# Decoder layer on one core: the SwiGLU up-projection by eight block products, or by seven

## The reference

```python
h = rms_norm(x, g_ffn[l])
u = h @ w_up[l]                      # (256, 2048) @ (2048, 11264)
up = jnp.pad(u, ((0, 0), (CONV_WIDTH - 1, 0), (0, 0)))
conv = sum(wc[t] * up[:, t:t + s] for t in range(CONV_WIDTH)) + b_conv[l]   # 3 taps along the tokens
gate, val = jnp.split(conv, 2, axis=-1)                                      # 5632 columns each
x = x + (jax.nn.silu(gate) * val) @ w_down[l]                                # (256, 5632) @ (5632, 2048)
```

## Time and profile before

| | |
|---|---|
| median of three runs | 1414.6 us |
| profiled execution, first to last instruction | 1413.1 us |
| PE busy | 1405.8 us (99%) |
| DVE busy | 890.7 us (63%) |
| ACT busy | 722.2 us (51%) |
| POOL busy | 53.0 us (4%) |
| moved by DMA | 265.97 MB, 188 GB/s on the mean |

### The profile page before, as it was taken

How to read it: one execution, slowest core, us unless ns; L and a number is a source line. 1 busy time by engine, 2 the same in 40 slices (tenths; PEclk the granted TensorE clock), 3 DMA queues, 4 the chain that set the end, 5 groups by cost and what they waited for, 6 DMA issues and landing times.

```text
span 1413.1 us, 19396 instructions
## 1 busy us (share of the span) xinstructions
PE 1405.8 (99%) x6947; PEld 1184.9 (84%) x6947; DVE 890.7 (63%) x1109; ACT 722.2 (51%) x884; POOL 53.0 (4%) x65
## 2 busy tenths in 40 slices
PE   8999999999999999999999999999999999999999
PEld 7888888888888888888888888888888888888887
DVE  5646455655454456555577767676767676776765
ACT  6655444464545444444555554555454645554551
POOL 0112111110000000000000000000000000000000
PEclk9999999999999999999999999999999999999999
DMA  9865555556666655756566666666666665656652
GB/s 332 257 188 162 160 160 167 170 165 189 181 188 183 189 188 187 239 182 194 176 194 182 198 185 187 190 189 189 188 185 193 179 195 176 203 170 206 178 191 93
DMA packets 138441, 265.97 MB, mean 188 GB/s; under 512 B 10528, under 2 KB 10784, under 8 KB 137888
## 3 DMA queue, kind: packets, MB, share of 16 engines
q1 hardware_dynamic: 135488, 262.36, 60.7%
q10 hardware_dynamic: 2912, 3.06, 0.7%
HBM read 263.29 MB, written 2.10 MB: 188 GB/s over the span
## 4 chain that ended last, share of the span: by engine, by line
PE 99%; DMA 0%; DVE 0%; SPq 0%; ACT 0%; issue 0%
PE acc L327 22%; PE acc L307 20%; PE acc L309 20%; PE acc L308 20%; PE acc L324 12%; PE acc L323 1%; PE acc L348 0%; PE acc L336 0%; PE acc L359 0%; PE acc L375 0%; DMA raw<-w_in 0%; PE acc L368 0%; PE acc L437 0%; PE acc L376 0%; PE acc L356 0%; PE acc L362 0%
## 5 line engine op out<-in xcount | busy, mean ns | idle before, releaser
L815 DVE TENSOR_TENSOR w_lo<-raw,w_hi 128x1024 fp32r<-128x1024 f32 x487 | 593.7, 1224 | 466.5 <-ACT w_hi L568 463.6
L568 ACT ACTIVATE w_hi<-raw 128x1024 fp32r<-128x1024 f32 x487 | 513.5, 1058 | 558.9 <-PE acc L309 372.6
L327 PE MATMUL acc<-actB,w_hi 128*128 128x512 f32 x1320 | 466.9, 398 | 0.0
L307 PE MATMUL acc<-w_hi,actA 128*128 128x512 f32 x1116 | 442.3, 396 | 2.0 <-DVE w_lo L815 2.0
L309 PE MATMUL acc<-w_hi,actA 128*128 128x512 f32 x1116 | 435.1, 390 | 0.0
L308 PE MATMUL acc<-w_lo,actA 128*128 128x512 f32 x1116 | 434.4, 389 | 0.0
L324 PE MATMUL acc<-actB,w_lo 128*128 128x256 f32 x1408 | 391.9, 281 | 0.0
L327 PEld LDWEIGHTS acc<-actB,w_hi 128*128 128x128 f32 x1320 | 248.0, 188 | 60.4
L324 PEld LDWEIGHTS acc<-actB,w_lo 128*128 128x128 f32 x1408 | 265.9, 189 | 2.0
L309 PEld LDWEIGHTS acc<-w_hi,actA 128*128 128x128 f32 x1116 | 209.5, 188 | 44.4
L307 PEld LDWEIGHTS acc<-w_hi,actA 128*128 128x128 f32 x1116 | 209.7, 188 | 43.7 <-issue 2.4
(11 more groups left out here) (141 smaller groups left out, 591.6 us busy)
## 6 DMA issues: line engine op xcount, KB each, us to landing
raw<-w_up SPq DMA_DIRECT2D x176, 512.0 KB, 4.2
raw<-w_in SPq DMA_DIRECT2D x159, 512.0 KB, 3.9
raw<-w_down SPq DMA_DIRECT2D x88, 512.0 KB, 4.5
raw<-w_out SPq DMA_DIRECT2D x32, 512.0 KB, 4.5
raw<-w_fox SPq DMA_DIRECT2D x16, 512.0 KB, 4.5
raw<-w_dil SPq DMA_DIRECT2D x16, 512.0 KB, 4.5
work<-x_t SPq DMA_DIRECT2D x8, 256.0 KB, 6.7
work<-x SPq DMA_DIRECT2D x2, 1024.0 KB, 8.9
```

What stands on the lines that cost most here:

```text
L307: nc.tensor.matmul(o, lhsT=a_h, rhs=w_hi[:, u, k, :], start=first and k == 0, stop=False)
L327: mm = nc.tensor.matmul(banks[j][:, :], lhsT=hi_w, rhs=actB[:, kt, :], start=False, stop=kt == KT - 1)
L568: nc.scalar.activation(w_hi[:, u, :, :], raw[:, u % RAW_SLOTS, :].rearrange("p (k n) -> p k n", k=KU), ACT.Copy).then_inc(hi_done, 1)
L815: nc.vector.tensor_tensor(w_lo[:, u, :, :], raw[:, u % RAW_SLOTS, :].rearrange("p (k n) -> p k n", k=KU), w_hi[:, u, :, :].bitcast(f32), A ...
```

## The change

The up-projection of a block is one product of 2 by 2 blocks. On the left stands the normalised input without its per-token factor, cut into two halves of tokens and two halves of the 2048 inner elements (A11, A12, A21, A22, each 128 by 1024). On the right stand four weight blocks of 1024 by 512: B11 and B21 (value columns, first and second half of the inner elements), B12 and B22 (gate columns). The seven products of Strassen's method, in the order of the new `step` 0 to 6, take A11, A12, S1, S4, S2, S3 and A22 on the left, where S1 to S4 are sums of the A blocks, made once. The weight sums on the right are made in place: SP loads B11 into `raw` and B21, later B22, into the new `raw_y`, and POOL issues DMAs that add a further block to what lies in the buffer (`accum_op=ALU.add`), for the steps 2, 4, 5 and 6. PE keeps on accumulating in the same PSUM bank over several steps, where the method allows it; ACT copies intermediate sums out (`p1_copied`, `p15_copied`, `p6_copied`), and DVE makes the four results of a block (`result`).

A unit of such a step ("S") has 6 matmuls of 512, with 128 tokens as the stationary operand, so that the tokens now lie on the partitions. The results are turned by 8 PE transposes for the gate and 8 for the value (`turn_up`), and all three taps are taken from PSUM. The down units ("D", 12 matmuls as before) are placed between the S units by a list, `ffn_units`. A block has 28 S and 8 D units: 36 weight units pass through `high` and `low` where 24 did. The D unit (i, 0) stands before S unit 12 of block i + 1. The first block has no D unit beside it, and after the last S unit 13 D units are left. The ring of split weights holds 6 units (`RING`), was 8. The whole program is unrolled. The arrays `w_up` and `w_down` are laid out so that a unit is contiguous, 4 KB on each partition. The last four attention heads no longer have their queries and values copied by POOL, and ACT's function tables are loaded once for the whole FFN, where before a block had two loads.

```diff
+STEPS = 7
+QU = HK // KU
+EARLY = (1, 4, 7)
+LATE = (12, 16, 20, 24, 26)
+LAST_LATE = 3
+X_STEPS = (0, 2, 4, 6)
+Y_STEPS = (1, 3, 5)
+
...
+def ffn_units():
+
+
+    units = []
+    for i in range(BLOCKS):
+        for step in range(STEPS):
+            for q in range(QU):
+                t = QU * step + q
+                late = LATE if i < BLOCKS - 1 else LATE[:LAST_LATE]
+                if i > 1 and t in EARLY:
+                    units.append(("D", i - 2, UPR - len(EARLY) + EARLY.index(t)))
+                if i > 0 and t in late:
+                    units.append(("D", i - 1, late.index(t)))
+                units.append(("S", i, step, q))
+    units += [("D", BLOCKS - 2, u) for u in range(LAST_LATE, UPR)]
+    units += [("D", BLOCKS - 1, u) for u in range(UPR)]
+    return units
+
+
...
+            def load_b11(i, q):
+                sp.dma_start(raw[:, q, :], w_up[1, i, q, :, :]).then_inc(w_loaded[q], 16)
+
+            def load_b21(i, q):
+                sp.dma_start(raw_y[:, q, :], w_up[1, i, QU + q, :, :]).then_inc(y_loaded[q], 16)
+
+            def load_b22(i, q):
+                sp.dma_start(raw_y[:, q, :], w_up[0, i, QU + q, :, :]).then_inc(y_loaded[q], 16)
+
+            def load_down(k):
+                sp.dma_start(raw_d[:, k % 2, :], w_down[k // UPR, k % UPR, :, :]).then_inc(d_loaded[k % 2], 16)
...
+            for n, unit in enumerate(FFN, FF_UNIT):
+                if unit[0] == "D":
+                    k = UPR * unit[1] + unit[2]
+                    if k + 2 < UPR * BLOCKS:
+                        sp.wait_ge(lo_done, n)
+                        load_down(k + 2)
...
+                    load_down(0)
+                    load_down(1)
+                if step == 1:
+                    sp.wait_ge(lo_done, n)
+                    load_b22(i, q)
+                elif step == 5 and i + 1 < BLOCKS:
+                    sp.wait_ge(lo_done, n)
+                    load_b21(i + 1, q)
+                elif step == 6 and i + 1 < BLOCKS:
+                    sp.wait_ge(lo_done, n)
...
+            def product_unit(n, part, q, o, first):
+
+                pe.wait_ge(lo_done, n)
+                s = n % RING
                 for k in range(KU):
-                    kt = KU * u + k
-                    for j in range(CT):
-                        hi_w, lo_w = w_hi[:, u, k, j * P:(j + 1) * P], w_lo[:, u, k, j * P:(j + 1) * P]
-                        if kt == 0:
-                            nc.tensor.matmul(banks[j][:, :], lhsT=hi_w, rhs=actB[:, kt, :], start=True, stop=False)
-                        mm = nc.tensor.matmul(banks[j][:, SEQ:], lhsT=lo_w, rhs=actB[:, kt, 0:SEQ],
-                                              start=False, stop=False)
-                        if kt > 0:
-                            mm = nc.tensor.matmul(banks[j][:, :], lhsT=hi_w, rhs=actB[:, kt, :], start=False,
-                                                  stop=kt == KT - 1)
+                    kt = KU * q + k
+                    a_h, a_l = part[:, kt, 0:P], part[:, kt, P:2 * P]
+                    nc.tensor.matmul(o, lhsT=a_h, rhs=w_hi[:, s, k, :], start=first and kt == 0, stop=False,
+                                     skip_group_check=True)
+                    nc.tensor.matmul(o, lhsT=a_h, rhs=w_lo[:, s, k, :], start=False, stop=False,
+                                     skip_group_check=True)
...
+            def turn_up(rows, ready):
+
+                for j in range(CT):
+                    for r in range(RT):
+                        t = nc.tensor.transpose(bank[3 + j // 2][:, (j % 2) * SEQ + r * P:(j % 2) * SEQ + (r + 1) * P],
+                                                rows[r][:, j * P:(j + 1) * P], ident)
+                t.then_inc(ready, 1)
+
+            def turn_val(i):
+                pe.wait_ge(c11_done, i + 1)
+                pe.wait_ge(c21_done, i + 1)
+                pe.wait_ge(conv_done, 2 * i + 1)
+                turn_up(val, val_ready)
+
+            def turn_gate(i):
+                pe.wait_ge(c12_done, i + 1)
+                pe.wait_ge(c22_done, i + 1)
+                if i:
+                    pe.wait_ge(conv_done, 2 * i)
+                turn_up(gate, gate_ready)
...
+            def down_unit(n, i, u):
+                c = u // 2
+                if u == 0:
+                    pe.wait_ge(a_lo, i + 1)
+                if u % 2 == 0:
...
+            for n, unit in enumerate(FFN, FF_UNIT):
+                if unit[0] == "D":
+                    down_unit(n, unit[1], unit[2])
...
+                if step == 0 and q == 2 and i:
+                    turn_val(i - 1)
+                elif step == 6 and q == 0:
+                    turn_gate(i)
...
+            def high(n):
...
+                    src = raw_d[:, u % 2, :]
+                    act.wait_ge(d_loaded[u % 2], 16 * (4 * i + u // 2 + 1))
+                else:
+                    _, i, step, q = FFN[n - FF_UNIT]
+                    src = raw[:, q, :] if step in X_STEPS else raw_y[:, q, :]
+                    if step == 0:
+                        act.wait_ge(w_loaded[q], 16 * (FF_UNIT // RAW_SLOTS + i + 1))
+                    elif step in X_STEPS:
+                        act.wait_ge(x_summed[q], 16 * (3 * i + step // 2))
+                    elif step == 5:
+                        act.wait_ge(y_summed[q], 16 * (i + 1))
+                    else:
+                        act.wait_ge(y_loaded[q], 16 * (2 * i + (step + 1) // 2))
+                if n >= RING:
+                    act.wait_ge(used, n - RING + 1)
+                nc.scalar.activation(w_hi[:, n % RING, :, :], src.rearrange("p (k n) -> p k n", k=KU),
                                      ACT.Copy).then_inc(hi_done, 1)
...
+            for n, unit in enumerate(FFN, FF_UNIT):
+                high(n + RING)
...
+                if step == 0 and q == 0 and i:
+                    gate_silu(i - 1)
+                elif step == 0 and q == 3:
+                    act.wait_ge(used, n + 1)
+                    if i:
+                        act.wait_ge(val_ready, i)
+                    else:
+                        act.wait_ge(nrs_ready, 1)
+                    for r in range(RT):
+                        t = nc.scalar.activation(val[r], bank[0][:, :], ACT.Copy, scale=xrs2[:, r:r + 1])
+                    t.then_inc(p1_copied, 1)
+                    if i:
+                        newest_tap(i - 1, 1)
+                elif step == 1 and i == 0:
...
+                elif step == 2 and q == 0 and i:
+                    hidden_high(i - 1)
...
+                elif step == 6 and q == 1:
+                    newest_tap(i, 0)
...
+            def older_tap(i, side, tap):
+
+                q = 2 * i + side
+                ct = 4 * i + 44 * side
+                if tap == 1:
+                    dve.wait_ge(tap2, q + 1)
+                else:
+                    dve.wait_ge(tap1, q + 1)
+                lag = 2 - tap
+                for j in range(CT):
+                    t = nc.vector.scalar_tensor_tensor(
+                        out=conv[:, j, lag:SEQ], in0=bank[3 + j // 2][:, (j % 2) * SEQ:(j % 2 + 1) * SEQ - lag],
+                        scalar=smalls_sb[:, S_WC + 88 * tap + ct + j:S_WC + 88 * tap + ct + j + 1],
+                        in1=conv[:, j, lag:SEQ], op0=ALU.mult, op1=ALU.add)
+                t.then_inc(tap1 if tap else conv_done, 1)
...
+                nc.vector.scalar_tensor_tensor(out=part, in0=o, scalar=scale, in1=part, op0=ALU.mult, op1=ALU.add)\
+                    .then_inc(done, 1)
+
+            for n, unit in enumerate(FFN, FF_UNIT):
+                low(n + RING)
+                if unit[0] == "D":
+                    _, i, u = unit
                     if u % 2 == 1:
-                        add_down(FF0 + 3 + 3 * i, u // 2)
...
+                if step == 1 and q == 3:
+                    dve.wait_ge(used, n + 1)
+                    dve.wait_ge(p1_copied, i + 1)
+                    result(bank[1][:, :], xrs2[:, 0:1], val[0], c11_done)
...
+                elif step == 6 and q == 2:
+                    older_tap(i, 0, 1)
+                elif step == 6 and q == 3:
+                    dve.wait_ge(used, n + 1)
+                    result(bank[2][:, :], xrs2[:, 1:2], val[1], c21_done)
+                    older_tap(i, 0, 0)
+                elif step == 1 and q < 3 and i:
+                    if q < 2:
+                        older_tap(i - 1, 1, 1 - q)
+                    else:
+                        hidden(i - 1)
+                elif step == 2 and q == 1 and i:
+                    hidden_low(i - 1)
 
...
+            def add_up(step, i, q):
+
+                if step in X_STEPS:
+                    half, side = {2: (0, 0), 4: (1, 0), 6: (1, 1)}[step]
+                    nc.gpsimd.dma_start(raw[:, q, :], w_up[side, i, QU * half + q, :, :], accum_op=ALU.add)\
+                        .then_inc(x_summed[q], 16)
+                else:
```

(45 more changed lines are left out.)

673 lines of the change are left out of this document (353 added, 320 removed).

## The result

The changed kernel takes 1525.8 us on the median of five runs (1517.7 to 1526.8), against 1414.6 before: ratio 1.0774, 95% interval 1.0751 to 1.0798, slower by 111 us. The forecast was 1450, its range ended at 1535. The profiled execution is the quickest of the five; its span is 1515.9 us, 66.9 above the 1449.0 of the prediction's sum.

The account below looks back on a forecast made before the run. The DMA engines were to bound the FFN, at two transfers per adding DMA: 732.5 + 35.4 + 5.3 + 0.9 = 774.1 us, 35.9 more than 738.2. Span 1413.1 + 35.9 = 1449.0, runs 1450 us; range 1375 to 1535.

Parts of the forecast that it names:

- PE's work: FFN block on PE: 28 S units, 8 D units and two sets of transposes take 61.6 us, before 67.0.
- The wait for `a_lo`: Before D unit (i, 0), PE waits 5.3 us for DVE's `hidden_low`, ten times: 53 us.
- The price of an adding DMA: Weight sums in the FFN: an adding DMA costs two plain loads, each 1.32 us of all 16 engines.
- The block's DMA work of 68.6 us: FFN block on the DMA engines: 20 + 2 x 16 = 52 loads, 68.6 us, just above PE's 66.9.
- The rule that I had cited: Weight sums: an adding DMA reads two sources through one ring and runs at half a copy's rate, giving 774.1 us.
- POOL's issues: Issuing 16 adding DMAs takes POOL 6 to 35 us of a block, beside other work.
- PE's 61.6 + 5.3 = 66.9: FFN block on PE: 61.6 us of work plus 5.3 of waiting for `hidden_low`, just under the DMA engines' 68.6.
- which leaves 732.5: FFN's 572 loads, 755 us, less 10.6 ahead of it and 11.9 beside the last D units: 732.5 us.
- Block 0 and the tail: First block costs 14 us in all; behind the loads, 13 D units (35.4), one wait (5.3), last add (0.9).
- Every sign: New trace: S units 1.36 us, some ten `hidden_low` waits at 5 us, DMA share near 1, landings well above 4.2.
- additions at 2.3 transfers or more: Rival on the weight sums: at 2.3, 825 us of loads, 1520 us; 18%, including issue on POOL holding it up.
- The rival with single prices: FFN: the waits stay but the DMA engines don't bind, -59.8 + 53 + 14 = +7, 1422 us; chance 20%.

Follow-up runs that it names:

- e11: Changed kernel with plain loads for the adding DMAs, `hidden_high` and `hidden_low` earlier, down sums over three banks, one `add_down` behind `hidden_low`: 1438.4 us, ratio 1.016.
- e9: No layer: 16 plain loads, then twice a block's transfers, POOL's 16 adding beside SP's 20 plain: 275 GB/s, 3.81 us a pair.
- e8: No layer, DMAs alone: 32 plain loads of 512 KB by POOL, 32 adding ones, 32 plain by SP: 1.28 us plain, 2.50 adding.
- e1: Changed kernel with POOL's 176 adding DMAs made plain loads of the same bytes, sums left out: 1500.6 us, ratio 1.061.
- e13: Changed kernel with plain loads for the adding DMAs and sixteen extra matmuls in PE's wait for `hidden_low`, blocks 0 to 8: 1477.9 us, ratio 1.044.
- e6: Changed kernel, sums by DMA kept, DVE's older taps cut to one instruction of 8 columns per set: 1505.2 us, ratio 1.063.
- e7: Changed kernel with plain loads for the adding DMAs and DVE's older taps cut to one 8-column instruction per set: 1438.4 us, ratio 1.017.

## Why the prediction was wrong, step by step

- *PE's work* (61.6 us a block) held: an S unit is 1.36 us, and e11's block of 65.0 is 61.6 plus 1.79 and 0.4 of waiting, and 1.2 of odds and ends, low clock among them (granted clock 0.98).
- *The wait for `a_lo`*, forecast at 5.3 us ten times, is 4.29 nine times and 6.6 once. The mechanism and the size were right.
- *The price of an adding DMA*, two transfers, was right (1.95 alone). The block's DMA work of 68.6 us was 2.5 too much: at e9's pair and e8's plain load it is 66.1, since a plain load is 1.28 us and not 1.32, and a sum 2.50 and not 2.64. The rule that I had cited from the Trainium skill ("Collectives: The Full Stack", section on the bandwidth ceiling) stands there for the reducing step of a ring of cores; for an adding DMA on one core the 410 and 210 GB/s of e8 agree with it.
- *POOL's issues*: 16 x 0.87 us a block, hidden as said.
- **The step that failed** is the one that put "PE's 61.6 + 5.3 = 66.9" just under the DMA engines' 68.6 and then let the engines run without a pause, "which leaves 732.5". First, the path through PE was mis-sized: without any sum it is 71.1 us (e1), not 66.9. The prediction left out the low clock behind the wait, 1.4 to 2.9 us (22.6 us over nine waits by e13), a bank wait of 1.5 and 0.4 for the result. So the order of the two was wrong: PE's path at 71.1 lies above the DMA engines' 66.1, and sets most of the block. Second, near to each other the two don't give their maximum. The block is 72.3, 1.2 more than PE's path, and e6 and e7 show it larger: without the taps PE's path is 65.8 (e7), the engines' work 66.1, and the block with both 71.5 (e6). What the traces show of how is that sums pile up, urgent ones take turns with loads that have time, and POOL's queue is dry while slots are not free; how much of the 1.2 and 5.7 us each makes stays open.
- *Block 0 and the tail.* Ahead of the first wait for `hidden_low` PE waits 28 us (10.7 for sums that land 3.8 us apart ahead of ACT's copy, L950), and behind the last block 16.3, where 14 and one wait of 5.3 had been named. The engines' sum had room for neither.

The ledger of the 66.9 us: nine blocks of 72.3 in place of 68.6 are 33, of which PE's path of 71.1 makes 22.5. The other 34 lie before the first and after the last of these blocks. The median run is 9 us further from the forecast than the profiled one (75.8 against 67), at a granted clock of 0.964 to 0.966 in place of 0.971; what makes the executions differ was not looked into.

Every sign that the prediction had named for itself came out: S units of 1.36, ten waits of 4.3 to 6.6 us, a share near 1, landings of 7.9 and 9.4 us. They show that the mechanisms are there, not that they are all. That 1525.8 lies inside the stated range is luck: its upper end was there for additions at 2.3 transfers or more (1520 us), and they cost 1.95. The rival with single prices, 1422, was the worse miss: e1 is it, and took 1500.6. Whoever had priced e1's block right would have seen that the change loses without one adding DMA.
